# Expert layers of a two-layer decoder step: row and product turns moved from TensorE to VectorE, raw rows gathered with their root, slot 9 loaded first

## The reference

```python
def rms_norm(x, g):
    return x * lax.rsqrt(jnp.mean(x * x, axis=-1, keepdims=True) + EPS) * g
...
def expert_block(args):                 # 32 experts, each token goes to two of one group
    xblk, e = args
    hid = jax.nn.silu(xblk @ w_gate[e]) * (xblk @ w_up[e])     # 1024 -> 512
    return hid @ w_down[e]                                     # 512 -> 1024
...
h = h + hier_moe(rms_norm(h, norm_m[layer]), ...)
```

## Time and profile before

| | us |
|---|---|
| median of 3 runs (1522.5 to 1524.5) | 1524.02 |
| the profiled execution's own time | 1519.33 |
| its span in the profile | 1517.4 |
| TensorE busy | 1470.7 (97% of the span) |
| VectorE busy | 634.6 (42%) |
| ScalarE busy | 285.0 (19%) |
| GpSimd busy | 73.0 (5%) |
| all DMA queues | 484.54 MB, mean 319 GB/s |
| mean granted clock | 0.994 |

### The profile page before, as it was taken

One profiled execution on the slowest core, in us unless ns is written; L12 is line 12 of the kernel. 1 busy time (PEld: TensorE's weight loads), 2 busy tenths in 40 slices (PEclk: granted clock), 3 DMA queues, 4 the chain that ended last, 5 costly groups with the idle time before them and its releaser, 6 DMA issues. The chain is left out here.

```text
span 1517.4 us, 20326 instructions
## 1 busy us (share of the span) xinstructions
PE 1470.7 (97%) x7727; PEld 738.4 (49%) x7727; DVE 634.6 (42%) x1657; ACT 285.0 (19%) x746; POOL 73.0 (5%) x123
## 2 busy tenths in 40 slices
PE   9999999999999999999999998899999999999995
PEld 8787878667333333333334445657333333333331
DVE  3666566445323323224244235735232322433324
ACT  2424244214110101001001004523010100110101
POOL 0101010001000000000000000001000000000000
PEclk9999999999999999999999999999999999999998
DMA  7432324467999999999999036785999999999993
GB/s 232 137 116 75 116 78 143 187 230 308 417 430 431 428 429 433 430 428 426 426 427 368 19 126 257 268 343 204 412 429 431 430 429 431 431 430 426 427 426 157
DMA packets 101504, 484.54 MB, mean 319 GB/s; under 512 B 16410, under 2 KB 51134, under 8 KB 67634
## 3 DMA queue, kind: packets, MB, share of 16 engines
q1 hardware_dynamic: 96818, 478.90, 78.0%
q0 software_dynamic: 4320, 4.42, 0.8%
q10 hardware_dynamic: 288, 0.14, 0.0%
HBM read 483.77 MB, written 10.97 MB: 326 GB/s over the span
## 5 line engine op out<-in xcount | busy, mean ns | idle before, releaser
L2539 PE MATMUL moe_ps_gate<-slots,moe_xrT 128*64 128x512 f32 x1024 | 228.1, 596 | 8.5 <-DMA slots<-in_w_gate_e_dram 8.5
L2539 PE MATMUL moe_ps_up<-slots,moe_xrT 128*64 128x512 f32 x1024 | 226.8, 595 | 0.0
L2566 PE MATMUL moe_ps_y<-slots,router_inputs 128*64 128x512 f32 x960 | 212.6, 595 | 0.0
L2412 DVE TENSOR_TENSOR resid<-resid,moe_ps_x 128x512 f32<-128x512 f32 x60 | 41.3, 688 | 252.7 <-PE moe_ps_x L2582 252.7
L2539 PEld LDWEIGHTS moe_ps_up<-slots,moe_xrT 128*64 128x64 f32 x1024 | 71.2, 137 | 150.9 <-issue 138.7
L2539 PEld LDWEIGHTS moe_ps_gate<-slots,moe_xrT 128*64 128x64 f32 x1024 | 72.2, 137 | 137.9 <-issue 136.7
L966 PE MATMUL gdn_bank<-gdn_xT,slots 128*128 128x288 f32 x512 | 136.3, 410 | 0.7 <-ACT slots L485 0.7
L2566 PEld LDWEIGHTS moe_ps_y<-slots,router_inputs 128*64 128x64 f32 x960 | 66.3, 137 | 124.9 <-issue 124.6
L2203 ACT ACTIVATE moe_xrT<-moe_ps_x,router_inputs 128x128 f32<-128x128 f32 x128 | 36.5, 367 | 379.1 <-PE moe_ps_x L2520 363.5
L966 PEld LDWEIGHTS gdn_bank<-gdn_xT,slots 128*128 128x128 f32 x512 | 92.6, 190 | 22.8 <-issue 1.1
L2381 DVE TENSOR_TENSOR router_inputs<-router_inputs,moe_ps_up 128x512 f32<-128x512 f32 x32 | 22.0, 688 | 195.0 <-PE moe_ps_up L2539 195.0
(11 more groups left out here) (509 smaller groups left out, 1817.9 us busy)
## 6 DMA issues: line engine op xcount, KB each, us to landing
slots<-in_w_gate_e_dram SPq DMA_DIRECT2D x40, 2048.0 KB, 23.0
slots<-in_w_up_e_dram SPq DMA_DIRECT2D x40, 2048.0 KB, 22.8
slots<-in_w_down_e_dram SPq DMA_DIRECT2D x40, 2048.0 KB, 25.8
slots<-in_w_gate_e_dram SPq DMA_DIRECT2D x48, 1024.0 KB, 26.2
slots<-in_w_up_e_dram SPq DMA_DIRECT2D x48, 1024.0 KB, 26.6
slots<-in_w_down_e_dram SPq DMA_DIRECT2D x48, 1024.0 KB, 26.0
slots<-in_w_in_a_dram SPq DMA_DIRECT2D x16, 1024.0 KB, 5.8
slots<-in_w_kv_dram SPq DMA_DIRECT2D x4, 2048.0 KB, 20.6
```

What stands on the lines that cost most here:

```text
L2412: V.tensor_tensor(half, half, banks[i][:, :], ALU.add).then_inc(s["summed"], 1)
L2539: last = T.matmul(ps[64 * e:64 * e + 64, :], xgT[:, k, 64 * e:64 * e + 64], slots[:, slot[2 * n + e], 512 * k:512 * k + 512], start=(k == ...
L2566: last = T.matmul(ps_y[64 * e:64 * e + 64, h, :], hidT[:, k, 64 * e:64 * e + 64], slots[:, slot[4 + e], 1024 * k + 512 * h:1024 * k + 512 ...
```

## The change

In both expert phases:

- The eight row transposes and the four hidden transposes of groups 1 to 15 leave TensorE. VectorE turns them with 32 x 32 block transposes instead: one instruction takes four tiles of one 32 x 32 block position, so that a half of the rows needs 16, all rows 32, the hidden rows 16. Both sources are read with a step, `xg` now of eight floats (it holds raw rows), `hid` of four.
- ACT scales all eight tiles by the norm weights, in place (`rows_scaled`).
- The gathered rows are the raw residual. Their root stands behind each row as a 1025th float, is copied by POOL to `rcur` and enters as the factor of silu (ACT) and of the product with up (VectorE). For group 0 it is multiplied into `sel0`.
- `xn` is not made any more (ACT's three strided copies and two memsets on POOL go). SP stores the residual at the start of the phase and the roots as three stores of single floats when they are there.
- Slot 9 is free from the start, and piece 9 is asked for right after these stores and, in layer 1, pieces 4 and 5.
- TensorE's order becomes: gate, `sel_T`, up, four combines, the fifth combine, down. VectorE's: `hidden`, `hid_turned`, `rows_turned` of the next group, five adds, selection, output copy. The fourth combine uses the bank `ps_hid`, freed from the hidden turn.

```diff
@@ moe_phase
-        sb("late_slots", [128, SLOT_COUNT - 7, SLOT_COLS])
-        xn = sb("last_slot", [128, SLOT_COLS])[:, 0:NT * D_MODEL].rearrange("p (t d) -> p t d", t=NT)
+        sb("late_slots", [128, SLOT_COUNT - 6, SLOT_COLS])
+        low = sb("low", [128, SLOTS])
+        rcur = sb("rcur", [128, 1])
...
-        ps_sum = [flat_x[0], flat_x[1], ps_tab, ps_gate, ps_up]
+        ps_sum = [flat_x[0], flat_x[1], ps_tab, flat_hid, ps_up]
...
+        xgv = strided(xg)
+        hidv = hid.rearrange("p (c k) -> p k c", k=FT)
@@ sync
+            for t in range(NT):
+                sp.dma_start(xn_dram[128 * t:128 * t + rows[t], 0:D_MODEL], resid[0:rows[t], t, :]).then_inc(s["xn_stored"], 16)
             if layer:
                 m["prefetch"](sp, layer, (4, 5))
+            m["prefetch"](sp, layer, (9,))
+            sp.wait_ge(s["inverse"], 1)
             for t in range(NT):
-                sp.wait_ge(s["normed"], t + 1)
-                sp.dma_start(xn_dram[128 * t:128 * t + rows[t], :], xn[0:rows[t], t, :]).then_inc(s["xn_stored"], 16)
+                sp.dma_start(xn_dram[128 * t:128 * t + rows[t], D_MODEL:D_MODEL + 1], rstd[0:rows[t], t:t + 1], allow_slow_non_contiguous=True).then_inc(s["xn_stored"], 16)
             if layer == 0:
                 m["attn_inputs"](sp)
-            sp.wait_ge(s["xn_stored"], 16 * NT)
-            sp.wait_ge(s["gx_T"], 1)
-            m["prefetch"](sp, layer, (9,))
+            sp.wait_ge(s["xn_stored"], 16 * 2 * NT)
@@ gpsimd, gather
-                pool.indirect_dma_start(xg, None, xn_dram[:, :], bass.IndirectOffsetOnAxis(rows_in[:, :], 0),
+                pool.indirect_dma_start(xg_row, None, xn_dram[:, :], bass.IndirectOffsetOnAxis(rows_in[:, :], 0),
                                         bounds_check=T_ALL - 1, oob_is_err=False).then_inc(s["gathered"], 16)
+                pool.wait_ge(s["gathered"], n * 16)
+                pool.wait_ge(s["hidden"], n)
+                pool.sem_inc(s["waits_held"], 1)
+                P.tensor_copy(rcur[:, :], xg_row[:, D_MODEL:D_MODEL + 1]).then_inc(s["r_kept"], 1)
@@ scalar
-            act.wait_ge(s["inverse"], 1)
-            for t in range(NT):
-                r = rows[t]
-                A.activation(by_tile(xn[0:r, t, :]), strided(resid[0:r, t, :]), ACT.Copy, scale=rstd[0:r, t:t + 1]).then_inc(s["normed"], 1)
...
+            def rows_scaled(g):
+
+                for n in range(2):
+                    act.wait_ge(*((s["gx_half"], g), (s["gx_T"], g + 1))[n])
+                    for k in range(4 * n, 4 * n + 4):
+                        last = A.activation(xgT[:, k, :], xgT[:, k, :], ACT.Copy, scale=norm_T[:, k:k + 1])
+                    last.then_inc((s["gx0_kept"], s["gx1_kept"])[n], 1)
...
+                    act.wait_ge(s["r_kept"], g)
+                    A.activation(hid, ps_gate[:], ACT.Silu, scale=rcur[:, 0:1]).then_inc(s["silued"], 1)
...
             with act.Fori(1, LAST) as g:
+                silu(g)
                 sel_kept(g - 1, flat_hid)
-                silu(g)
-                rows_kept(g + 1)
+                rows_scaled(g + 1)
                 kept(g)
@@ vector
-                    last = V.tensor_scalar(sel0[:, t, SLOTS * e:SLOTS * e + SLOTS], low, pos0[:, t, e:e + 1], None, ALU.is_equal)
+                    last = V.tensor_scalar(sel0[:, t, SLOTS * e:SLOTS * e + SLOTS], low[:, :], pos0[:, t, e:e + 1], rstd[:, t:t + 1], ALU.is_equal, ALU.mult)
...
+            def blocks_turned(dst, src, ks):
+
+                for q in range(4):
+                    for a in range(4):
+                        last = V.transpose(dst[32 * q:32 * q + 32, ks, 32 * a:32 * a + 32], src[32 * a:32 * a + 32, ks, 32 * q:32 * q + 32])
+                return last
+
+            def rows_turned(g):
+
+                dve.wait_ge(s["gathered"], g * 16)
+                blocks_turned(xgT, xgv, slice(0, 4)).then_inc(s["gx_half"], 1)
+                blocks_turned(xgT, xgv, slice(4, KT)).then_inc(s["gx_T"], 1)
+
+            def hid_turned(g):
+
+                dve.wait_ge(s["hidden"], g + 1)
+                blocks_turned(hidT, hidv, slice(0, FT)).then_inc(s["hid_kept"], 1)
...
+                    V.scalar_tensor_tensor(hid, hid, rcur[:, 0:1], ps_up[:], ALU.mult, ALU.mult).then_inc(s["hidden"], 1)
...
             with dve.Fori(1, LAST) as g:
-                for i in range(3):
+                hidden(g)
+                hid_turned(g)
+                rows_turned(g + 1)
+                for i in range(5):
                     add(g - 1, i, ps_sum)
-                hidden(g)
-                turned(g)
-                for i in range(3, 5):
-                    add(g - 1, i, ps_sum)
-                rows_kept(g + 1)
                 selection(g, False, lpos, gcol[:, :, :, bass.ds(g, 1)].rearrange("p k t o -> p k (t o)"))
                 kept(g, s["y_made"])
@@ tensor, gate_up
-                pe.wait_ge(s["hid_kept"], g)
-                sel_T(g - 1, flat_hid)
                 pe.wait_ge(s["silued"], g)
-                if not (isinstance(g, int) and g == 1):
-                    pe.wait_ge(s["summed"], g * 8 - 12)
                 stage(g, 0, ps_gate, slot, filled)
-                outputs_kept(g - 1)
-                for i in range(3):
-                    combine(g - 1, i, ps_sum)
                 pe.wait_ge(s["hidden"], g)
                 if not (isinstance(g, int) and g == 1):
                     pe.wait_ge(s["summed"], g * 8 - 8)
+                sel_T(g - 1, flat_hid)
                 stage(g, 1, ps_up, slot, filled)
-                pe.wait_ge(s["silued"], g + 1)
-                combine(g - 1, 3, ps_sum)
-                hid_T(g)
+                outputs_kept(g - 1)
+                for i in range(4):
+                    combine(g - 1, i, ps_sum)
+                pe.wait_ge(s["hidden"], g + 1)
                 combine(g - 1, 4, ps_sum)
-                pe.wait_ge(s["summed"], g * 8 - 6)
@@ decoder_step
-    m["xn_dram"] = nc.dram_tensor("xn_rows", (T_ALL, D_MODEL), F32, kind="Internal").ap()
+    m["xn_dram"] = nc.dram_tensor("xn_rows", (T_ALL, D_MODEL + 1), F32, kind="Internal").ap()
```

More of the change, by code:

```diff
@@ L2260, in _ @@
                     V.tensor_copy(xrT[:, 4 * j:4 * j + 4, at[t]], ps_xT[t][:, j, :, 0:rows[t]]).then_inc(s["xT_kept"], 1)
-            link(V.tensor_scalar(low, m["lanes"][:, 0:SLOTS], BELOW, None, ALU.add))
+            link(V.tensor_scalar(low[:, :], m["lanes"][:, 0:SLOTS], BELOW, None, ALU.add))
             dve.wait_ge(s["roots"], 1)
@@ L2380, in hidden, with first_turned @@
                 dve.wait_ge(s["silued"], g + 1)
-                V.tensor_tensor(hid, hid, ps_up[:], ALU.mult).then_inc(s["hidden"], 1)
-            def turned(g):
-                dve.wait_ge(s["hid_T"], g + 1)
+                if isinstance(g, int) and g == 0:
+                    V.tensor_tensor(hid, hid, ps_up[:], ALU.mult).then_inc(s["hidden"], 1)
+                else:
+                    V.scalar_tensor_tensor(hid, hid, rcur[:, 0:1], ps_up[:], ALU.mult, ALU.mult).then_inc(s["hidden"], 1)
+            def first_turned():
+                dve.wait_ge(s["hid_T"], 1)
                 V.tensor_copy(hidT, ps_hid[:]).then_inc(s["hid_kept"], 1)
@@ L2512, in _ @@
                 T.matmul(ps_count, ones[0:rows[t], :], both[0:rows[t], t, :], start=(t == 0), stop=(t == NT - 1))
-            xgv = by_tile(xg)
-            hidv = hid.rearrange("p (c k) -> p k c", k=FT)
-            def rows_T(g):
-                pe.wait_ge(s["gathered"], g * 16)
-                for k in range(KT):
-                    last = T.transpose(ps_x[:, k // 4, k % 4, :], xgv[:, k, :], ident[:, :])
-                last.then_inc(s["gx_T"], 1)
             def landed(half, i, slot, filled):
@@ L2542, in stage, with first_hid_T @@
                         last.then_inc((half_used, used)[k // 4][n], 1)
-            def hid_T(g):
-                pe.wait_ge(s["hidden"], g + 1)
+            def first_hid_T():
+                pe.wait_ge(s["hidden"], 1)
                 for k in range(FT):
@@ L2624, in _ @@
                 for t in range(NT):
-                    last = T.matmul(ps_x[:, k // 4, k % 4, :], by_tile(xn[:, t, :])[:, k, :], sel0[:, t, :], start=(t == 0), stop=(t == NT - 1))
+                    last = T.matmul(ps_x[:, k // 4, k % 4, :], strided(resid[0:rows[t], t, :])[:, k, :], sel0[0:rows[t], t, :], start=(t == 0), stop=(t == NT - 1))
                 if k == 3:
@@ L2643, in _ @@
             last.then_inc(s["extras_made"], 1)
-            hid_T(0)
-            rows_T(1)
+            first_hid_T()
             products(0, slot, filled)
@@ L2649, in _ @@
             gate_up(1, slot, filled)
-            rows_T(2)
             products(1, slot, filled)
@@ L2657, in _ @@
                     gate_up(g, slot, later)
-                    rows_T(g + 1)
                     products(g, slot, later)
@@ L2662, in _ @@
                 gate_up(g, slot, filled)
-                rows_T(g + 1)
                 products(g, slot, filled)
             slot, filled = pieces(LAST)
```

(19 more changed lines are left out.)

70 lines of the change are left out of this document (32 added, 38 removed).

## The result

The changed kernel takes 1773.65 us (median of 4 runs, 1771.62 to 1776.61) against 1523.26 us (1521.36 to 1524.5): ratio 1.165, 95% interval 1.1625 to 1.1669, **250 us slower**. The profiled execution took 1772.85 us with a span of 1770.7, 0.8 us under the median. I had forecast slower, but by 31 us, and the range ended at 1608.

A forecast was written before the change was run, and what follows sets the result against it. TensorE and DMA were taken as both full. 30 x (28.9 - 27.5) = 42, less 8.5 for weight waits, plus 0.7 for starts, less about 1.5 per phase for group 0, gave +31 us: 1555; range 1523 to 1608.

The forecast's parts named there:

- the latency on VectorE binds: Expert groups: turns add 15.6 us a group to a VectorE 42% busy, so it has room, but latency binds.
- TensorE waits before down for VectorE and in gate for ACT: Each group: TensorE waits 1.9 us before down and some 1 us in the middle of gate.
- the weight waits of 8.5 us vanish: Gate's waits for weights in both phases' late groups vanish, as the DMA is no longer caught up with: minus 8.5 us.
- the early piece 9 is worth nothing: Phase start: piece 9 comes over 10 us earlier, but piece 10 still waits for the same half product: 0 us.
- rival C: Kernel 8's own expectation: the early tenth slot pays 4.9 us a phase back, total 1540 to 1545; no chance given.
- TensorE's own work is 25.9: Each group: TensorE loses 0.57 + 1.03 us of transposes from 27.49, leaving 25.9 us; alone worth nothing.
- I take t = 0.325: Time of one VectorE turn: 128 columns at ACT's stepped 1.95 ns plus 0.076 us overhead, 0.325 us for both sources.
- my upper bound of 0.38: Longest VectorE turn, taking its slope to double as ACT's more than did: 0.38 us, p = 31.5 and +109 us.
- Now the cycle that closes on itself: Group period from end of up through hidden, 48 turns, scaling, half gate, `sel_T`, up: 13.3 + 48 t, 28.9 us.
- no clock loss worth telling: Main forecast case: t 0.30 to 0.35 and no notable fall of TensorE's granted clock; chance 0.45.
- The two starts at 0.7 us: Start of both phases: a second scalar on six `sel0` operations, +0.36 us per phase; stores, copies and gather 0.
- turns dearer, or the clock joins in: Rival: t = 0.349 plus one clock fall per group from waits before down (+20 us), +86 us: 1610; chance 0.25.

The follow-up runs named there:

- kernel 8: Against the changed kernel, all turns are on TensorE again; raw rows, root factors, stepped picks and early piece 9 stay: 1550.1 us.
- Run 1: Against the changed kernel, the 48 turns read dense 128-column blocks instead of stepped floats, giving other outputs: 1629 us.
- run 2: Against the changed kernel, the 48 turns are plain copies through the same stepped views, giving other outputs: 1591 us.
- run 3: Against the changed kernel, the row turns are 16 instructions of 256 columns instead of 32 of 128: 1753.7 us.
- Run 4: Against the changed kernel, TensorE turns the previous group's selection (`sel_T`) behind up instead of between gate and up: 1745.1 us.
- Run 5: Against the changed kernel, three extra 512-column matmuls fill most of TensorE's wait before down: 1759.8 us.
- run 9: Against kernel 8, eight extra 128-column matmuls in TensorE's 0.94 us wait before the stepped picks of group 0: 1549.8 us.
- run 10: Against run 9, the picks of group 0 load a dense instead of a stepped stationary operand, giving other outputs: 1533.1 us in one run.
- run 7: Against the changed kernel, the silu product is turned on TensorE again, behind the last combine; the 32 row turns stay on VectorE: 1706.9 us.
- 11: Against run 7, the four transposes of the silu product stand directly behind the first combine instead of the last: 1633.6 us.
- run 12: Against run 11, the selection's turn (`sel_T`) moves behind up, with the four transposes of the silu product right behind it: 1567.6 us.
- run 6: Against the changed kernel, the picks of group 0 load dense 128-column blocks instead of every eighth float: 1769.4 us in one run.

## Why the prediction was wrong

*Right.* It is slower; the latency on VectorE binds and not its share of busy time; TensorE waits before down for VectorE and in gate for ACT; the weight waits of 8.5 us vanish; the early piece 9 is worth nothing, as kernel 8 shows (rival C of its expectation, 1540 to 1545, did not come). "TensorE's own work is 25.9" is not contradicted, it is never reached.

The sum was 31 us, 250 were measured. The prediction fails at four steps, here with what each was short by. The first two are the main ones: t, and the cycle.

1. *"I take t = 0.325", 128 us.* The spacing is 0.414, above my upper bound of 0.38: (0.414 - 0.325) x 48 x 30. In that figure I charged the stepped read by ACT's price (0.113 us in 128 columns) and the turning nothing. Run 1 puts the step at 0.097 on a turn, run 2 the turning at 0.133 on a stepped read. My overhead of 0.076 us an instruction was also too small: run 3 puts it at 0.18 for a turn. ACT's row was the wrong relative to borrow from, and an upper bound made of one suspected cost is no upper bound when the operation itself is unseen. My estimate from the page that I cited (the Trainium skill, Vector Engine (DVE) Microarchitecture Reference, 5.2 Measured stream behaviour) was 0.30 to 0.395; the measurement is above that too. Its 1.73 ns a column for one stepped source is near the 1.80 of run 3; its 75 ns an instruction is not the 180 here. The rule of the Trainium skill (SBUF — State Buffer, Door 1: The DMA port swizzle) that a step of up to four floats is free is not borne out for VectorE's turns here: 0.317 us dense, 0.409 at four floats, 0.414 at eight.

2. *"Now the cycle that closes on itself", 13.3 + 48 t, 53 us.* I followed VectorE's turns into ACT's scaling and stopped there. In VectorE's own order the adds and the selection stand behind the turns, and `sel_T`, which the change moved in front of up, waits for them. That is the moved step whose queue I had not walked to its end: 15.1 + 48 t, 1.8 us a group more. Run 4 takes this link away, groups fall to the 32.6 that the shorter chain gives where the clock holds, and the total falls by 29 as it mostly doesn't.

3. *The clock, 14 us.* I priced it as a rival at 20 and left it out of the sum ("no clock loss worth telling"). Run 5 measures 14. It follows the waits: where one wait goes, as in run 4, the clock falls behind the next.

4. *The two starts at 0.7 us, measured 26.* I costed the stores, the copies, the gather and a second scalar, and not the 48 picks themselves, whose stationary operand became stepped. Run 8 isolates it: 26.4 us. Runs 9 and 10 show the stepped load as the bound, with the fallen clock behind it in tab (2.90 instead of 1.53) and gate (9.47 instead of 7.09).

These four add up to 128 + 53 + 14 + 25 = 220, and with the 31 to 251; that this meets the 250 so closely is in part luck, as the terms are not clean. Read straight off the two profiled spans, 1770.7 against 1517.4, the 30 stretches from up to up are 210 us longer, the two starts (first turn of the residual to end of up of group 0) 29, and what follows the last up of each layer 15. The first stretch of each layer lasts 28.7 and 30.4 us and not 34.95, and the 15 us at the ends stand in no step of mine.

The rival "turns dearer, or the clock joins in" (1610) named two of the causes and had a third of the size. That a mechanism on VectorE decides was right: runs 7, 11 and 12 take groups from 34.95 to 27.4 us without making a single turn faster. The range failed by t already: 0.414 in my own cycle gives 31 + 128 = 159, so 1683. The cycle of step 2 and the start of step 4, which all its cases shared, did the rest.

## What to carry to other kernels

When work moves onto an engine that runs in order, write down its whole list for one turn of the loop and, for each item, who waits for it. The period is the longest cycle through that list, and what stands behind the moved work counts as much as the work (run 12 hides 32 turns of 0.414 us, run 7 with the same turns loses 33.03 - 27.4 = 5.6 us a group). Cost an operand whose layout changes wherever it is read, also in the one place outside the loop. An operation that no trace shows needs a bound for itself beside one for its access.

## What the runs showed of the hardware

- A 32 x 128 f32 turn on VectorE follows the last at 0.317 us from dense and 0.414 us from stepped rows; one of 256 columns at 0.645.
- A stationary f32 operand of 128 columns read with a step of eight floats loads in 330 ns at a clock of 1.00 as at 0.50 (run 9). A dense one takes 190 at 1.00 (run 10).
- Forty-eight matmuls with such stepped loads take 15.5 to 16.1 us (run 9, run 8). The clock was 1.00 when they began and fell during them, also in run 9, where TensorE had no idle time before them or in them.
- Whether the clock falls turned on small differences. With dense picks it fell behind a wait of 0.94 us (run 6) and held at 1.00 when that wait was filled (run 10). In the kernel before it held behind a wait of 0.67 us, with picks that all had 128 rows. In two groups of the changed kernel one after the other, a wait of 2.38 us in gate was followed by 0.50 and one of 2.37 by 1.00.
